# Gate products with the turns inside, one output column split ahead, and shifts and weight rests handed to GpSimd, in a two-model kernel on one core

## What is computed

```python
# first model, each layer: 16 experts on 64 tokens (and, in the first layer, 32 context tokens)
hid = silu(xs @ wg) * (xs @ wu)
ys  = hid @ wd                       # scattered back with the gates

# first model, second layer: the shifts and the first of six mixes
xx = h_shift - h                     # four quarters of the channels: left, right, up, down
xr, xw, xk, xv, xa, xg = [h + xx * mix[j] for j in range(6)]
wlog = w0[d] + tanh(xw @ w1[d]) @ w2[d]      # d = 0, 1

# second model, each of two layers
uv, z, xbc, dt_raw, c_q, c_kv, k_rope = split_cols(rmsnorm_2(x, g) @ w_in[l])
```

## Time and profile before

| | us |
|---|---|
| median of 3 runs | 3729.87 |
| lowest and highest | 3729.07, 3737.04 |
| profiled execution | 3728.67 |
| its span in the profile | 3726.4 |
| TensorE busy | 3445.3 |
| VectorE busy | 1474.0 |
| ScalarE busy | 1102.0 |
| GpSimd busy | 283.7 |

### The profile page before, as it was taken

How to read it: one execution, slowest core, us unless ns; L and a number is a source line. 1 busy time by engine, 2 the same in 40 slices (tenths; PEclk the granted TensorE clock), 3 DMA queues, 4 the chain that set the end, 5 groups by cost and what they waited for, 6 DMA issues and landing times.

```text
span 3726.4 us, 64269 instructions
## 1 busy us (share of the span) xinstructions
PE 3445.3 (92%) x28700; PEld 2265.4 (61%) x28700; DVE 1474.0 (40%) x2582; ACT 1102.0 (30%) x2076; POOL 283.7 (8%) x242
## 2 busy tenths in 40 slices
PE   6999999999899999999779887899999999999998
PEld 4555344334457588888433332266888876778886
DVE  2232001013532267777540000147753435674343
ACT  4131111112442255554210000134532323543131
POOL 0000000000000234444100000000000000000000
PEclk9989999999799999999989999999999999999999
DMA  9246988996434344331528999920242312133320
GB/s 350 81 162 271 359 328 323 370 348 241 145 124 158 91 99 85 85 71 43 182 113 343 421 413 421 420 87 18 74 147 91 98 44 75 41 114 111 92 91 23
DMA packets 340515, 666.54 MB, mean 179 GB/s; under 512 B 156600, under 2 KB 250296, under 8 KB 284944
## 3 DMA queue, kind: packets, MB, share of 16 engines
q1 hardware_dynamic: 330128, 633.14, 47.2%
q10 hardware_dynamic: 6912, 18.88, 1.3%
q0 software_dynamic: 3200, 10.42, 0.8%
HBM read 630.92 MB, written 31.46 MB: 178 GB/s over the span
## 4 chain that ended last, share of the span: by engine, by line
PE 75%; DVE 9%; DMA 8%; ACT 3%; POOL 2%; issue 1%; SPq 1%; DVEq 0%; ACTq 0%; POOLq 0%
PE ps L1054 14%; PE ps L1059 5%; DMA ring<-in_moe_wu 4%; PE ps L693 4%; PE ps L3163 3%; PE ps L3162 3%; PE ps L3161 3%; PE ps L3179 3%; PE ps L3180 3%; PE ps L3178 3%; PE ps L609 2%; PE ps L610 2%; PE ps L611 2%; PE ps L1483 2%; PE ps L1508 2%; POOL ring L1855 2%
## 5 line engine op out<-in xcount | busy, mean ns | idle before, releaser
L1054 PE MATMUL ps<-ring,H 128*64 128x512 f32 x2016 | 480.3, 598 | 36.9 <-DMA ring<-in_moe_wu 32.5
L1163 DVE TENSOR_TENSOR scr<-ps,scr 128x512 f32<-128x512 f32 x32 | 22.1, 691 | 910.1 <-PE ps L1059 504.6
L1054 PEld LDWEIGHTS ps<-ring,H 128*64 128x64 f32 x2016 | 142.8, 136 | 319.2 <-issue 244.3
L1054 PE MATMUL ps<-ring,scr 128*64 128x512 f32 x1016 | 245.9, 602 | 32.1 <-DMA ring<-in_moe_wd 28.0
L3143 DVE TENSOR_TENSOR ring_rounded<-ring,scr_rounded 128x2048 fp32r<-128x2048 f32 x64 | 146.7, 2292 | 216.6 <-ACT scr_rounded L3136 216.3
L3178 PE MATMUL ps<-scr_rounded,ring_rounded 128*128 128x512 f32 x512 | 201.8, 394 | 1.6 <-DVE ring_rounded L3143 1.6
L3161 PE MATMUL ps<-scr_rounded,ring_rounded 128*128 128x512 f32 x512 | 202.8, 396 | 0.0
L3163 PE MATMUL ps<-scr_rounded 128*128 128x512 f32 x512 | 202.6, 396 | 0.0
L3180 PE MATMUL ps<-scr_rounded 128*128 128x512 f32 x512 | 202.4, 395 | 0.0
L3162 PE MATMUL ps<-H_rounded,scr_rounded 128*128 128x512 f32 x512 | 202.3, 395 | 0.0
L3136 ACT ACTIVATE scr_rounded<-ring 128x2048 fp32r<-128x2048 f32 x64 | 122.2, 1909 | 242.7 <-PE ps L3180 242.7
(11 more groups left out here) (519 smaller groups left out, 6768.1 us busy)
## 6 DMA issues: line engine op xcount, KB each, us to landing
ring<-in_moe_wu SPq DMA_DIRECT2D x128, 1024.0 KB, 8.3
ring<-in_moe_wd SPq DMA_DIRECT2D x127, 1024.0 KB, 9.2
ring<-in_moe_wg SPq DMA_DIRECT2D x124, 1024.0 KB, 8.7
ring<-in_mlp_w SPq DMA_DIRECT2D x64, 1024.0 KB, 5.4
ring<-in_ada_w SPq DMA_DIRECT2D x48, 1024.0 KB, 11.8
ring<-in_w_in SPq DMA_DIRECT2D x14, 1024.0 KB, 5.4
ring<-in_w_out SPq DMA_DIRECT2D x8, 1024.0 KB, 5.6
st_kka<-scr ACTq DMA_DIRECT2D x16, 384.0 KB, 3.5
```

What stands on the lines that cost most here:

```text
L1054: ins = pe.matmul(bx[64 * n:64 * n + 64, :], stat_x(k), w[:, k % 4, :], start=k == 0, stop=k == KT - 1)
```

## The change

Four edits, with no change to what is computed. (1) The turn of the expert before moves from ahead of the gate product to between its two halves. (2) The upper parts of the first part of output column 0 are made before the last expert's results are read out on ScalarE. (3) In `n1`, four of the modulation blocks move on TensorE into the loop over k of `lw`, whose two segments now alternate; ScalarE does all shifts first and the modulation after; shift and first mix alternate tile by tile on VectorE, and the shifts of tiles 5 to 7 are done by GpSimd. (4) In the second model the rests of `xbc.0` to `xbc.2` are done by GpSimd behind its loads, VectorE's wait for the constants comes after its first four splits, and `yh` keeps its slot until `ckv`, by which nine entries of the plan stand in other slots.

```diff
+LASTS["yh"] = "i0.ckv"
...
-        def split_low(dve, name):
+        def split_low(eng, name, e="V", done=vector_done):
...
-        def rest_high(act, m):
+        def rest_high(act, m, n):
+            x0, x1, c0, c1 = parts_of(m)[n]
...
                         for n in range(2):
                             marks[f"wf.w{nm}{i}.{e}.0.{n}"] = (T_, count[T_])
+                        if between:
+                            between()
...
-                if e:
-                    turn(e - 1)
-                first("g")
+                first("g", (lambda: turn(e - 1)) if e else None)
...
             turned(NE - 1)
             if i == 1:
                 gated_high(act, 6)
+            else:
+                rest_high(act, 0, 0)
             out(NE - 1)
...
-            for m in range(3):
-                rest_high(act, m)
+            rest_high(act, 0, 1)
+            rest_high(act, 1, 0)
+            rest_high(act, 2, 0)
...
+                banks = {s0: bank(pe, f"{tag}.{s0}") for s0, sn in jsegs(j)}
+                for k in range(KT):
+                    if later(pe, f"xj{j}.{k}"):
+                        pe.wait_ge(*at(f"xj{j}.{k}"))
+                    for s0, sn in jsegs(j):
+                        ins = pe.matmul(banks[s0][:, 0:sn], w[:, k, :], of[:, k, s0:s0 + sn], start=k == 0, stop=k == KT - 1)
+                        if k == KT - 1:
+                            did(T_, ins.then_inc(tensor_done, 1), f"{tag}.{s0}")
+                    if between:
+                        between(k)
...
+            down("lw", "w1", 1, None, between=lambda k: ada_tensor(pe, ADA_N1[0] + 3 + k, ADA_N1[0] + 4 + k == ADA_N1[1]) if ADA_N1[0] + 3 + k < ADA_N1[1] else None)
...
+        def shifted(eng, e, done, k):
+            def sub(out_, a_, b_):
+                did(e, eng.tensor_tensor(out_, a_, b_, ALU.subtract).then_inc(done, 1))
+            def neg(out_, in_):
+                did(e, eng.tensor_scalar(out_, in_, -1.0, None, ALU.mult).then_inc(done, 1), None)
...
+            elif k < 6:
+                sub(to[:, 64:TX], h[:, 0:TX - 64], h[:, 64:TX])
+                neg(to[:, 0:64], h[:, 0:64])
...
+        XX_POOL = (5, 6, 7)
...
             for k in range(KT):
+                if k not in XX_POOL:
+                    shifted(dve, V, vector_done, k)
+                if k:
+                    first_mix(k - 1)
+            first_mix(KT - 1)
...
         def rw_pool(pool):
+            for k in XX_POOL:
+                shifted(pool, G_, pool_done, k)
...
             marks[f"mlac{l}"] = ("aux", count["aux"])
+            for n in range(3):
+                split_low(pool, f"i{l}.xbc.{n}", G_, pool_done)
...
         def mla_vector(dve, l):
             t0 = f"i{l}."
-            if later(dve, f"mlac{l}"):
-                dve.wait_ge(*at(f"mlac{l}"))
             hk = f"n2{l}"
             split_low(dve, f"{t0}cq.1")
             mean_vector(dve, hk, MEAN, MEAN1)
             split_low(dve, f"{t0}ckv")
             split_low(dve, f"{t0}kr")
+            if later(dve, f"mlac{l}"):
+                dve.wait_ge(*at(f"mlac{l}"))
...
-                    shift_scalar(act, st, SEGS, lambda k: ada_scalar(act, ADA_N1[0] + 2 + k, ADA_N1[0] + 3 + k == ADA_N1[1]) if ADA_N1[0] + 2 + k < ADA_N1[1] else None)
+                    shift_scalar(act, st, SEGS)
+                    for b in range(ADA_N1[0] + 2, ADA_N1[1]):
+                        ada_scalar(act, b, b == ADA_N1[1] - 1)
```

More of the change, by code:

```diff
@@ L905, in parts_of @@
             return ((0, 7, 0, 3), (7, 8, 3, 4)) if m == 0 else ((0, 8, 0, 4),)
-        def rest_high(act, m):
+        def rest_high(act, m, n):
+            x0, x1, c0, c1 = parts_of(m)[n]
             o = slice(m * P, m * P + P)
[L910 to L915, removed]
+            for step in [f"yg.{x1 - 1}", f"yg.{7 + c1}", "free.pb0.c3"] + ([f"mo0.{m - 3}.{TX}"] if m >= 3 else []):
+                if later(act, step):
+                    act.wait_ge(*at(step))
+            did(A_, act.activation(RHX[m % 3][:, x0:x1, :], YSX[:, x0:x1, o], ACT.Copy).then_inc(scalar_done, 1))
+            did(A_, act.activation(RHC[m % 3][:, c0:c1, :], YSC[:, c0:c1, o], ACT.Copy).then_inc(scalar_done, 1), f"rh.{m}.{n}")
         def rest_low(dve, m, n):
@@ L1439, in xj, with down @@
                 return lambda k, s0, sn: XJ[:, k, s0:s0 + sn]
-            def down(tag, wn, j, last_name, of=XJ):
+            def down(tag, wn, j, last_name, of=XJ, between=None):
                 w = weight(pe, wn)
[L1443 to L1449, removed]
+                banks = {s0: bank(pe, f"{tag}.{s0}") for s0, sn in jsegs(j)}
[8 more added lines that the diff above has]
+                        between(k)
                 marks["wf." + wn] = (T_, count[T_])
                 marks[f"xjfree{j}"] = (T_, count[T_])
-            down("lw", "w1", 1, None)
+            down("lw", "w1", 1, None, between=lambda k: ada_tensor(pe, ADA_N1[0] + 3 + k, ADA_N1[0] + 4 + k == ADA_N1[1]) if ADA_N1[0] + 3 + k < ADA_N1[1] else None)
             w = weight(pe, "w2")
@@ L1524, in rw_tensor @@
             marks["wf.g2"] = (T_, count[T_])
-        def rw_vector(dve):
[L1529 to L1533, removed]
-            for k in range(KT):
[L1535 to L1555, removed]
-                    neg(XX[:, k, TA - 1:TA], H[:, k, TA - 1:TA])
-            dve.wait_ge(*own(dve, V))
@@ new lines, in build, with first_mix @@
+        XX_POOL = (5, 6, 7)
+        def rw_vector(dve):
+            def first_mix(k):
+                j = order[0]
+                if later(dve, f"xx.{k}"):
+                    dve.wait_ge(*at(f"xx.{k}"))
+                did(V, dve.scalar_tensor_tensor(XJ[:, k, :], XX[:, k, :], col("mix", 8 * j + k), H[:, k, :],
+                                                ALU.mult, ALU.add).then_inc(vector_done, 1), f"xj{j}.{k}")
+            for k in range(KT):
+                if k not in XX_POOL:
[3 more added lines that the diff above has]
+            first_mix(KT - 1)
@@ L1568, in mix @@
                                                     ALU.mult, ALU.add).then_inc(vector_done, 1), f"xj{j}.{k}")
-            mix(0)
             for d in range(2):
```

43 lines of the change are left out of this document (30 added, 13 removed).

## The result

The changed kernel takes 3710.93 us (median of 4 runs, 3707.20 to 3715.87); the kernel before took 3729.47 in the same comparison (median of 4). The ratio is 0.9947 with a 95% interval of 0.9935 to 0.9959: faster by some 19.8 us (15 to 24). The forecast was 3723, with 3708 to 3736 as its range. The sign of the largest terms and their places were right; the size of the gain was three times what I forecast.

What follows compares the result with a forecast made beforehand. TensorE, busy 92% of the span, bounds the kernel; -10.3 (turns) -4.6 (first column) +15.5 (`rw`) -3.9 -3.3 (`mla` layers) = -6.6 takes 3728.67 to 3722.1, a median of 3723 us, range 3708 to 3736.

Steps and rivals of the forecast that it cites:

- Turns: Expert borders: nine TensorE waits for the turn go in `moe0`, -10.3 us; `moe1` counted as 0.
- First column: Spread products after the last down product in `moe0`: column 1 starts at 905.9, not 910.47, -4.6 us.
- The late start of GpSimd: `n1` and `lw`: GpSimd waits for block 47's read-out, starts at 981.5, and `zw` starts 8.8 us later.
- The clock in zw: `rw`: the first half of `zw` runs at half clock after TensorE stood mostly idle, +8.6 us.
- the allowance: `rw`: 1.9 us taken off because TensorE's pauses further on shrink, leaving +15.5 for `rw`.
- Rival A: `zw` keeps full clock in its first half: `rw` costs only 6.9, total -15.2, about 3714; chance 0.20.
- mla, first layer: Third latent product 6.5 us earlier, but GpSimd's splits hold VectorE up by 8.3: -3.9 for the layer, not -10.0.
- mla, second layer: The 1.95 wait for the constants goes and 1.4 of the first softmax wait: -3.3 us together.
- B: GpSimd does not hold VectorE up in `mla`: layers give -10.0 and -3.8, total -13.2, 3716; chance 0.11.
- C: `rw` costs nothing, as GpSimd starts early: total about -22, 3707; chance 0.07.

Runs made afterwards that it cites:

- the run alone: The kernel before with only the turns moved inside the gate product; 3715.58 us against 3728.14, ratio 0.9959.
- The early mark: The changed kernel with ScalarE's mark of `n1` set behind its eight shifts, not behind the read-out of block 47; 3701.03 us, ratio 0.9924.
- the second mix spread: The changed kernel with all shifts on VectorE and the second mix spread behind the first eight decays of `zw`; 3688.31 us, ratio 0.9888.
- the blocks back: The changed kernel with all shifts on VectorE and the four modulation blocks back in `n1`; 3690.39 us, ratio 0.9893.

## Why the prediction came out as it did

**Turns.** -10.3 by nine waits of 1.1, -10.8 in the trace; nothing in `moe1`, as `moe_wg`'s wait rose from 4.2 to 10.3 where 7.1 had been saved. Right, by its reasons; shown by the run alone.

**First column.** -4.6, measured -3.9. The path (read-out, second part, column 1) is the one described; column 1 started 7.7 us behind the last down product where I had 8, and before the change it was 12.5. What is missing of the 4.6 is half clock for the eight instructions from 894.66 on, behind a wait of 1.84. No run tests it by itself, but the stretch is 3.9 to 4.0 us shorter in all traces with this edit and 0.5 in the two without.

**The late start of GpSimd.** The step that the diff hides was right in place and size: GpSimd waited for block 47, and `zw` started 8.4 us later where I had 8.8. Its start at 966.52, with the 14.9 us added that the trace was ahead, is 981.4; I had 981.5. The early mark shows the cause: some 6 of the 8.4 go with it.

**The clock in zw.** This step failed. It said that "TensorE has stood mostly idle for 12 us ahead of `zw`" and so its first half runs at half clock: +8.6 (+6.7 with the allowance). It measured -0.8. The idle stretch was shorter (one wait of 3.54), and behind it the steps of `lw` ran at half clock, 2.7 us each, just about as slow as GpSimd's tiles came, every 2.9: so TensorE had no gap to speak of in the 7.1 us of the last three steps and was back at 2.4 GHz before `zw`. I had priced only the last of these steps, at 0.9, had not followed the two before it, and so called a stretch idle that was not. Rival A was that case, and rightly named; its chance of 0.20 was too small. The rule of the Trainium skill (TensorE: Matmul & The Clock Gate, part 1), that the throttled state is the default and activity releases it, agrees with the rise at 976; what I had wrong was the activity. It does not account for the 23.9 us at 0.50 from 993.5 on, in which TensorE was busy 22.60. The allowance of 1.9 for later pauses came to nothing apart from this.

**mla, first layer.** The 6.5 us up to the third latent product are 6.7. The holding-up of VectorE was right in kind: two splits of 4.87 and 4.51 (4.6 forecast), 7.3 us lost (8.3 forecast). The first softmax came 5.1 us earlier by the entry to the layer, not 3.9, and the first turned block with it. What I missed is what follows on TensorE: before, it ran at 0.50 behind the wait of 4.73, and now it keeps 1.00 behind the 1.40, which is another 2.1. So the layer gave 7.3 and not 3.9. The rule that I named from the Trainium skill (SBUF — State Buffer, section on the two separate sides), that of a VectorE operation with two SBUF inputs and a GpSimd one the later is fully blocked, agrees with the step of 0.68 that took 3.70. The price named from the Trainium skill (GPSIMD Engine Reference, section 3.1), 4497 ns for 2048 columns, agrees with the 4.51 of the second split; the first took 4.87. With the rests left on VectorE this layer still gave 6.9, so nearly all of its 7.3 comes from the kept slot and the later wait, and the move bought nothing here.

**mla, second layer.** -3.3, measured -3.8: the 1.95 gone, and 3.67 down to 2.06, a gain of 1.6 where I had 1.4.

**The sum.** 19.1 against 6.6: of the 12.5 between, the clock in `zw` is 7.5, the first `mla` 3.4, and the rest the small terms. That the result, 3710.93, lay inside the range was luck in part. A held, and with the rest of the sum it gives 3714. B did not hold, as VectorE was held up by 7.3 us, though part of its gain came for another reason. The lower edge of 3708 was set by C, `rw` for nothing, and C was false: `rw` cost 7.6 us.

## What to carry to other kernels

When work is handed to another engine, look at what its position in the program waits for, not only at its data: here a stage mark that stood behind another engine's side work cost most of 8 us, and setting it earlier gave some 6 of them back. Keep the pieces of work that an idle engine does ahead of time short: one of 7.5 us, on an engine at 40% load, made a pause of 1.8 us on TensorE, and the pause was followed by over 20 us at half clock. Price a step at both clocks before calling the time around it idle; a step that is slow enough fills its gap.

## What the runs showed of the hardware that I had not expected

A pause of 1.96 us in front of `zw` left the clock at 1.00 in the changed kernel, with all shifts on VectorE and with the second mix spread. A pause of 1.83 in the middle of `zw` was followed by 0.50 in every run that had it, although TensorE was busy nearly all of that time: 23.9 us in the changed kernel, busy 22.60, and 27.2 in the kernel before:

```profile
998.20:1025.40 27.20, 26.61 (x39) 12.69 (x40) 6.75 (x12) 12.61 (x24) 4.03 (x8) 0.50 0.64 238
```

With the blocks back, where the 1.96 came behind waits of 0.24 and 0.40 in `lw`, the clock fell within `zw` all the same, from 967.3 to 984.3. What makes the one pause harmless and the other dear, and what ends the half clock sooner in one than in the other, no run here settles.
